# Where the attention outputs are split in the first block, and how layer norm's mean reaches all rows

## What is computed

```python
    gated = jnp.concatenate([ya * jax.nn.silu(ag), yb * jax.nn.silu(bg),
                             yc * jax.nn.silu(cg), ym * jax.nn.silu(mg)], axis=-1)
    y = gated @ w_out
    alpha = (2.0 * DEPTH) ** 0.25
    return _layer_norm(alpha * x + y, ln_gain, ln_bias)

def _layer_norm(x, g, b, eps=1e-5):
    xf = x.astype(jnp.float32)
    mu = jnp.mean(xf, axis=-1, keepdims=True)
    var = jnp.mean(jnp.square(xf - mu), axis=-1, keepdims=True)
    y = (xf - mu) * lax.rsqrt(var + eps) * g.astype(jnp.float32) + b.astype(jnp.float32)
    return y.astype(x.dtype)
```

## Time and profile before

| | us |
|---|---|
| median of three runs | 1739.89 |
| lowest and highest run | 1737.13, 1739.97 |
| the profiled execution | 1740.3 |
| its span | 1738.5 |
| PE busy in it | 1668.4 |
| DVE, ACT, POOL busy | 786.5, 695.0, 683.6 |

### The profile page before, as it was taken

The page is one execution under the profiler, slowest core; times in us unless marked ns, Lnnn a source line. Parts: engine busy times, 40 slices in busy tenths (PEclk is TensorE's granted clock), DMA queues, the critical chain, the costliest instruction groups (busy, mean ns, idle before and its releaser), DMA issues.

```text
span 1738.5 us, 23836 instructions
## 1 busy us (share of the span) xinstructions
PE 1668.4 (96%) x8754; PEld 1320.4 (76%) x8754; DVE 786.5 (45%) x1498; ACT 695.0 (40%) x1146; POOL 683.6 (39%) x523
## 2 busy tenths in 40 slices
PE   6999899999999979989999999999998999999999
PEld 5777668787666857868888888888876888888887
DVE  7216664402666265673544115523665355404440
ACT  4344462633445153553433224333454344313431
POOL 3432315343231544425444444344352544344433
PEclk9999999999998979989999999999999999999999
DMA  6321203222120213112222232224221322232222
GB/s 248 107 80 49 80 25 122 96 100 74 50 75 26 85 49 103 51 50 97 97 97 78 91 108 88 91 79 138 86 74 41 105 77 94 90 103 97 97 81 88
DMA packets 26879, 150.68 MB, mean 87 GB/s; under 512 B 3888, under 2 KB 4144, under 8 KB 12912
## 3 DMA queue, kind: packets, MB, share of 16 engines
q1 hardware_dynamic: 23968, 142.78, 24.3%
q10 hardware_dynamic: 2832, 6.84, 1.1%
HBM read 142.66 MB, written 2.10 MB: 83 GB/s over the span
## 4 chain that ended last, share of the span: by engine, by line
PE 85%; DVE 6%; ACT 3%; issue 3%; POOL 2%; DMA 1%; ACTq 0%; DVEq 0%; POOLq 0%
PE ring L554 72%; PE outs L616 3%; PE scores L602 2%; PE ring L602 1%; POOL w_lo L540 1%; PE scores L626 1%; PE ring L640 1%; PE ring L626 1%; PE ring L670 1%; DMA xt<-in_x 1%; DVE tmp L1505 1%; POOL w_fold L532 1%; ACT xt L1267 1%; ACT w_hi L1049 1%; DVE probs_t L1531 0%
## 5 line engine op out<-in xcount | busy, mean ns | idle before, releaser
L540 POOL TENSOR_TENSOR w_lo<-w_stage,w_hi 128x258 fp32r<-128x258 f32 (+5 forms) x471 | 650.0, 1410 | 1010.8 <-ACT w_hi L1049 610.5
L554 PE MATMUL ring<-xh,w_lo 128*128 128x512 f32 x1296 | 519.6, 401 | 19.2 <-DVE w_lo L1463 10.7
L554 PE MATMUL ring<-xh,w_hi 128*128 128x512 f32 x1296 | 514.1, 397 | 0.0
L554 PE MATMUL ring<-xl,w_hi 128*128 128x512 f32 x1296 | 513.8, 396 | 0.0
L554 PEld LDWEIGHTS ring<-xh,w_lo 128*128 128x128 f32 x1296 | 245.5, 189 | 80.7 <-DVE w_lo L1463 10.7
L554 PEld LDWEIGHTS ring<-xh,w_hi 128*128 128x128 f32 x1296 | 246.1, 190 | 55.7
L554 PEld LDWEIGHTS ring<-xl,w_hi 128*128 128x128 f32 x1296 | 246.0, 190 | 53.3
L1394 ACT ACTIVATE w_hi<-w_stage 128x2048 fp32r<-128x2048 f32 (+2 forms) x70 | 116.6, 1666 | 158.2 <-PE ring L554 158.2
L1404 ACT ACTIVATE g<-ring,convw 128x512 f32<-128x512 f32 x88 | 68.1, 778 | 245.4 <-DVE ring L1903 245.4
L1049 ACT ACTIVATE w_hi<-w_stage 128x2064 fp32r<-128x2064 f32 (+2 forms) x81 | 123.4, 1536 | 64.9 <-PE ring L554 64.4
L1885 DVE TENSOR_TENSOR xt<-xt,ring 128x512 f32<-128x512 f32 x48 | 33.0, 688 | 247.3 <-PE ring L554 247.3
(11 more groups left out here) (281 smaller groups left out, 2213.4 us busy)
## 6 DMA issues: line engine op xcount, KB each, us to landing
w_stage<-in_mixed SPq DMA_DIRECT2D x62, 1032.0 KB, 4.8
w_stage<-in_up SPq DMA_DIRECT2D x44, 1024.0 KB, 4.8
w_stage<-in_down SPq DMA_DIRECT2D x16, 768.0 KB, 4.3
w_stage<-in_down SPq DMA_DIRECT2D x16, 640.0 KB, 3.9
xt<-in_x ACTq DMA_DIRECT2D x4, 512.0 KB, 11.4
g<-q SPq DMA_DIRECT2D x16, 128.0 KB, 2.3
out_t<-xt ACTq DMA_DIRECT2D x8, 256.0 KB, 2.0
mem_f<-in_mem SPq DMA_DIRECT2D x1, 1024.0 KB, 9.6
```

Source lines behind the costliest of these rows:

```text
L540: ins = nc.gpsimd.tensor_tensor(w_lo[:, slot, cols], source[:, cols], w_hi[:, slot, cols].bitcast(F32), ALU.subtract)
L554: ins = nc.tensor.matmul(o, lhs, rhs, start=start, stop=stop, skip_group_check=True)
```

## The change

```diff
@@ ring_plan
-        take(*[("mk", l + 1, 0)] * ahead, ("mean", l), ("mean_bc", l), *[("mk", l + 1, 1), ("mv", l + 1, 0)] * ahead, ("var", l), ("ln_bc", l),
+        take(*[("mk", l + 1, 0)] * ahead, ("mean_bc", l), *[("mk", l + 1, 1), ("mv", l + 1, 0)] * ahead, ("var", l), ("ln_bc", l),
@@ TensorE
-                mean(("mean", l), 0, [g[:, 0, :]], after("res_sum", (KD - 1) * (l + 1) - 1))
-                pe.wait_ge(S("mean_in"), l + 1)
-                spread(("mean_bc", l), stat, 0)
+                o = acquire(("mean_bc", l))
+                pe.wait_ge(S("res_sum"), (KD - 2) * (l + 1))
+                nc.tensor.matmul(o[:, :], ones[:, 0:1].to_broadcast([P, P]), g[:, 0, :], start=True, stop=False, skip_group_check=True)
+                wait_taken(pe, ("wout", l, KD - 1))
+                nc.tensor.matmul(o[:, :], ones[:, 0:1].to_broadcast([P, P]), xt[:, KD - 1, :], start=False, stop=True,
+                                 skip_group_check=True).then_inc(S("ring_full"), 1)
@@ ScalarE
+                    yield from until(66)
                     for n in range(7):
-                        yield from until(62 + n // 2)
                         split_out(l, n)
@@ VectorE
                     for n in range(7):
-                        yield from until(62 + n // 2)
+                        yield from until(66 + 2 * ((n + 1) // 2))
                         out_lo(l, n)
@@ VectorE
-                    if k >= 1:
+                    if 1 <= k < KD - 1:
...
                         if k >= 2:
-                            dve.wait_ge(S("res_sum"), (KD - 1) * l + k - 1)
+                            dve.wait_ge(S("res_sum"), (KD - 2) * l + k - 1)
                         v.tensor_tensor(g[:, 0, :], xt[:, 0, :] if k == 1 else g[:, 0, :], xt[:, k, :], ALU.add).then_inc(S("res_sum"), 1)
-                wait_full(dve, ("mean", l))
-                step(v.tensor_copy(stat[:, 0:4], bank(("mean", l))[:, 0:4]))
-                dve.sem_inc(freed(("mean", l)), 1)
-                dve.sem_inc(S("mean_in"), 1)
```

## The result

| | kernel before | changed kernel |
|---|---|---|
| median of its runs | 1739.93 us (6 runs, 1737.13 to 1744.77) | 1731.34 us (6 runs, 1729.01 to 1734.22) |
| span of the profiled execution | 1738.5 us | 1731.5 us |
| TensorE's mean granted clock in it | 0.978 | 0.982 |

The medians differ by 8.6 us. The ratio by all the runs is 0.9942, with a 95% interval of 0.9924 to 0.9960: 10.1 us less, between 7 and 13. The profiled execution of the changed kernel took 1733.3 us. In what follows W is the start of the first output product, and the *tail* is the time from the third query tile's scores (384 columns) to W.

The account below looks back on a forecast made before the run. TensorE was taken as the bound, busy 1668.4 of 1738.5 us. Terms -3.67 + 0.35 - 6.17 - 2.9 + 1.43 = -10.96 us gave 1729.3 us for this execution, 1729.0 us as median; range 1726.0 to 1735.3.

Parts of the forecast that it names:

- Splits, layer 0: End of block 1's attention: without four low parts ahead of the masks, the first output product starts 3.67 us earlier.
- What is now late: Moved high and low parts, last gating and eighth low part at block 1's end: all covered, nothing waits there.
- The next weights: Chunk 14 of the output weights comes later than TensorE wants it: +0.35 us in layer 0, nothing in layer 1.
- Splits, layer 1: End of block 1's attention: at full clock it takes layer 0's new 10.82 us instead of 16.99, 6.17 us less.
- Mean, layer 1: Layer norm: two 512-column products replace small products, copy and transposes; first subtraction 2.9 us earlier, bounds 2.0 and 3.4.
- Mean, layer 0: Layer norm: 0.2 us earlier for DVE, worth nothing, since the variance products start behind POOL's chunk.
- The ring: PSUM bank plan loses a name; block 2's layer 0 head sums wait for DVE to empty v's bank: +1.43 us.
- The clock did not fall again: Rival, chance 0.15: the clock falls again in the tails of block 1's attention, losing 3.4 to 10.2 us; 1733 us.
- The masks were what held the tail: Rival, chance 0.12, claimed they were not: only TensorE's idle time goes and the clock's fall stays; 4.9 us gain, 1735.0.
- The product with a repeated column: Rival, chance 0.08: the new mean's product is slow; at twice its price the mean saves 1.2 us, 1731.
- The bank's wait: Rival, chance 0.08: the bank's wait at block 2's head sums is hidden; 1727.6 us.
- The slower rival: Chance 0.05: TensorE's three new waits let the clock fall before dense products, 5.1 us each, together 15; 1744 us.

Follow-up runs that it names:

- e5_filled_gap: Kernel before with nine unused 512-column products filling TensorE's idle gap ahead of the fourth tile's scores; 1738.84 us against 1740.32, ratio 0.9988.
- e13_mean_again: Second profile of the kernel before with the new mean and its bank plan, splits as before; one run, 1739.34 us, beside 1737.08.
- e2_mean_only: Kernel before with the new mean and the bank plan it brings, splits as before; 1740.74 us against 1741.13, ratio 1.0002.
- e7_banks_best: Changed kernel with two places skipped in the bank rotation between the two blocks; 1729.77 us against 1740.32, ratio 0.9938.
- e11_chunk_first: Changed kernel with banks moved on by two and ACT rounding chunk 14 ahead of the eighth high part; 1735.37 us against 1740.67, ratio 0.9964.

## Why the prediction was right, and where it was not

The median came out 2.3 us above the forecast, inside the range. The steps for the splits, the new products and the bank were right; that the number came so near is in part luck, as the sum below shows. Point by point:

*Splits, layer 0: forecast 3.67 us, measured 3.46.* The 512-column scores start exactly where the reference pair put them, 2.81 us behind the others. Behind them the first mask and the third tile's copies came 0.1 us later than reckoned, and the product with the values 0.2.

*What is now late.* The eighth high part followed the last gating at W + 2.46 (forecast: gating ends at about W + 2.7), nothing waited for a low part, and the last copies were not held up.

*The next weights: forecast +0.35 us in layer 0, measured +0.16.* The gap is there (0.33 us). POOL ended at W + 11.05, not 11.33. In layer 1 W to the last update grew by 0.03, as forecast.

*Splits, layer 1: forecast 6.17 us, measured 5.95 in the two profiles, but about 3.5 in the kernel.* **This is the term that failed.** The step "if the clock stays full, it takes layer 0's new 10.82 us in place of 16.99" was right in its first half. Its second half took a low stretch of 10.2 us, seen once, for the kernel's steady state. Four other profiles show 14.3 to 14.6. The prediction had the warning in its own rows: layer 0 ran the same instructions in 14.49.

*Mean, layer 1: forecast 2.9 us, measured 2.84, and about 1.85 in the kernel,* by the same fault: the 4.75 us of the earlier trace rows is 3.75 in all five other profiles. The price of the new products was right.

*Mean, layer 0: forecast nothing, measured 0.6 us.* The first subtraction comes 0.14 us earlier. The stretch behind it ("norm 0") was 17.1 to 17.4 us in six profiles with the old mean, but 15.6 to 15.8 in five and 17.0 in three with the new one; the shorter form has 3.4 us at the lower clock in it, the longer one 6.8. Most of that is no gain, since TensorE then waits about 0.3 us for DVE ahead of each of the later operands of the next projection. What is left at "tile 2" is 25.34 us with the old mean in all six, 24.80 in five and 24.90 to 25.14 in three with the new one, by the means 0.5 us. Timeline of the kernel before, then of the changed kernel's second profile:

```profile
310.62 5.61 POOL L540 TENSOR_TENSOR w_lo<-w_stage,w_hi 128x258 fp32r<-128x258 f32 x8 [4.94 <-ACT w_hi L1049]
...
313.14 2.48 DVE L1710 TENSOR_TENSOR xt<-xt,ring 128x512 f32<-128x512 f32 x4 [0.91 <-PE ring L679]
...
315.54 1.24 DVE L1688 TENSOR_TENSOR g<-g 128x512 f32<-128x512 f32 x1
...
324.64 1.12 PE L679 MATMUL ring<-ident,rtok 128*128 128x128 f32 x4 [1.79 <-DVE rtok L1717]
...
338.48 0.39 PE L554 MATMUL ring<-xh,w_lo 128*128 128x512 f32 x1
```

```profile
305.83 6.06 POOL L540 TENSOR_TENSOR w_lo<-w_stage,w_hi 128x258 fp32r<-128x258 f32 x8 [4.94 <-ACT w_hi L1052]
...
308.21 2.48 DVE L1709 TENSOR_TENSOR xt<-xt,ring 128x512 f32<-128x512 f32 x4 [3.88 <-PE ring L904]
...
310.61 0.70 DVE L1691 TENSOR_TENSOR g<-g 128x512 f32<-128x512 f32 x1
...
333.01 0.39 PE L554 MATMUL ring<-xh,w_lo 128*128 128x512 f32 x1
```

The step "the variance products start behind POOL's chunk" was true and did not decide: TensorE waited 1.79 us behind these products, for rtok, which comes through DVE's subtractions and additions and ACT. In that chain DVE's first addition of squares took 1.23 to 1.25 us in all six profiles with the old mean, where POOL's last piece of the chunk had started about 0.05 us ahead of it and took 0.73 to 0.76. The 0.14 us turned this round: in all eight with the new mean the addition starts 0.1 us ahead of POOL's last piece and takes 0.69 to 0.71 us, and POOL's piece takes 1.17 to 1.19 (its whole chunk 6.06 us instead of 5.61).

*The ring: forecast +1.43 us, measured +1.42,* as the only edit +1.43, and gone in both kernels that undo it. That this shift also spares layer 1's tail 0.67 us was missed, though without effect on the sum, which took the new banks as they are.

*The rivals.* The clock did not fall again in the tails: it was full in both tails of all eight profiles that have the moved splits, in spite of the transposes. The rule of the Trainium skill ("TensorE: Matmul & The Clock Gate", Part 4: PE-mode transpose) that a transpose does not count as busy like other products made a fall the likelier. The trace does not agree as far as these tails go: 18 of their 50 products are transposes, and no fall came. How much a transpose counts no run here shows. The masks were what held the tail (e5_filled_gap: 2.84 of 3.5 us). The product with a repeated column cost what a score product costs. The bank's wait was not hidden. The slower rival asked for falls behind the new waits. There is none in the tails and none behind chunk 14. Behind the head sums' 1.36 us none came in any profile.

*The sum again, with the typical sizes:* -3.5 - 3.5 + 0.2 - 0.1 - 1.85 + 1.43 = -7.3 us, and -7.8 with the 0.5 us of "tile 2". The medians differ by 8.6 and 9.6 us, and -7.8 lies near the lower end of both intervals. Two distances in which neither part of the change stands also differ between the means of the eight profiles with the new mean and the six with the old, and they cancel: "m", 42.7 us in five of six and 41.1 in seven of eight, is 1.1 us shorter, and "mid 2" is 1.1 us longer. Ahead of the table's first distance the profiles differ by up to 4.8 us (layer 0's 384-column scores start between 247.8 and 252.6). So the two oversized terms were together 3.7 us too large, 0.5 us came that was not forecast, and what brought the medians nearer to the forecast than this the runs do not show.

*What stays open.* Why "m" favours its short form with the new mean. The long form has a low stretch behind a gap of 1.26 us that both forms have. Windows over 640 to 670 of the kernel before, and of e13_mean_again:

```profile
640.00:670.00 30.00, 28.38 (x120) 0.94 0.35 106
```

```profile
640.00:670.00 30.00, 28.71 (x130) 1.00 0.40 117
```

One kernel made both (e2_mean_only the long one, e13_mean_again the short one), and e5_filled_gap has the short one with the old mean. It is a draw with odds that the change seems to move; the odds rest on 14 profiles and no mechanism. The same holds for "mid 2": its four longest are four of the five profiles with the short "norm 0".

## What to carry to other kernels

Price a stretch with a fallen clock only after a second profile, or after its twin in another layer, and put the difference between twins into the range, not into the forecast. Work that nobody needs yet belongs behind the masks and maxima on their engine; if its reader takes operands one by one, most of it can wait until the reader has started, but not beside an engine that slows it. A product that starts earlier is a gain only as far as the operands behind it come earlier too, so measure to a later start. After any name leaves a ring of banks, compare each name's predecessor on its bank for both the waits that come and those that go: here one of 1.43 us came, and one of 0.67 us would have come without the shift.

## What the runs showed of the hardware

- **The clock falls behind the same gap in one execution and not in the next.** In the latent stage of layer 1 TensorE waits 2.1 us in every profile. The clock stayed full behind that in six of the fourteen, stood low for 6.8 us in four and for 10.2 us in four. Behind the gap of about 2.2 us in the old tails it fell every time. Timeline rows of the gap, then the windows, of the changed kernel and of e7_banks_best:

```profile
487.71 0.47 PE L554 MATMUL ring<-lat_h,w_lo 128*96 128x512 f32 x1 [2.08 <-ACT vb L1119]
```

```profile
483.05 0.74 PE L555 MATMUL ring<-lat_h,w_lo 128*96 128x512 f32 x1 [2.09 <-ACT vb L1120]
```

```profile
480.00:495.00 15.00, 12.59 (x84) 1.00 0.20 72
```

```profile
480.00:495.00 15.00, 12.91 (x48) 0.66 0.19 70
```

  The column "mid 2" shows what it costs: 211.5 to 211.7 us in the six, 214.5 to 214.7 with 6.8 us at the lower clock, and 216.0 to 216.1 with 10.2. That is 3.0 and 4.4 us, more than most edits here are worth, and may be a part of the scatter of one kernel's runs (1735.5 to 1750.4 us for the kernel before, in three measurements).
- **DVE and POOL slow each other.** Three subtractions of DVE with both inputs in SBUF took 2.99 us where two of them ran beside POOL's subtractions and 1.89 us alone; POOL's eight pieces took 6.84 and 5.67 us. Where only one instruction of each overlaps, in layer 0's norm, the later one paid: DVE's addition 1.24 instead of 0.70 us, or POOL's piece 1.18 instead of 0.75, and 0.14 us of DVE's time decided which. The Trainium skill ("SBUF — State Buffer", Who interferes with whom) says that a DVE instruction with two SBUF inputs contends with a GpSimd instruction that reads SBUF, and the trace agrees, with about 1.1 us on each side in e11_chunk_first.
